# A fused two-model block on one core: the first microseconds and the last block of rows rearranged

## The reference

```python
h = h + 0.5 * swiglu(rms_norm(h, ffn1_norm[li]), ffn1_wi[li], ffn1_wo[li])   # the first FFN, from x
...
x = x + FFN_RESIDUAL_WEIGHT * swiglu_2(rms_norm_2(x, ffn2_norm[l]),          # the last FFN, its result is returned
                                     ffn2_w_gate[l], ffn2_w_up[l], ffn2_w_down[l])
```

## Time and profile before

| what | value |
|---|---|
| median of 3 runs | 1520.33 us |
| profiled execution | 1519.9 us |
| its span, first to last instruction | 1518.1 us |
| mean granted PE clock | 0.993 |
| PE busy | 1486.0 us (98%) |
| DVE busy / ACT busy | 876.0 us (58%) / 710.2 us (47%) |

### The profile page before, as it was taken

One profiled execution on the slowest core, in us unless ns is written; L12 is line 12 of the kernel. 1 busy time (PEld: TensorE's weight loads), 2 busy tenths in 40 slices (PEclk: granted clock), 3 DMA queues, 4 the chain that ended last, 5 costly groups with the idle time before them and its releaser, 6 DMA issues.

```text
span 1518.1 us, 16928 instructions
## 1 busy us (share of the span) xinstructions
PE 1486.0 (98%) x7061; PEld 1234.9 (81%) x7061; DVE 876.0 (58%) x1040; ACT 710.2 (47%) x834; POOL 84.6 (6%) x101
## 2 busy tenths in 40 slices
PE   8999999999999999999799999999999889999999
PEld 6888888888888888888688888888888768888887
DVE  6465456565545655459765554755547786765543
ACT  6444345554434444344554444543436666354432
POOL 0000012000000000006000000000000440000000
PEclk9999999999999999999999999999999999999999
DMA  9555472365555655544455556565556342555552
GB/s 315 177 184 177 133 258 98 130 199 189 194 167 194 194 180 188 173 147 153 138 182 193 173 175 207 181 192 183 180 169 207 124 165 86 194 179 189 187 180 70
DMA packets 143890, 265.66 MB, mean 175 GB/s; under 512 B 7070, under 2 KB 24950, under 8 KB 143558
## 3 DMA queue, kind: packets, MB, share of 16 engines
q1 hardware_dynamic: 141974, 259.11, 52.0%
q0 software_dynamic: 1104, 4.35, 0.9%
q10 hardware_dynamic: 736, 1.12, 0.2%
HBM read 263.52 MB, written 1.05 MB: 174 GB/s over the span
## 4 chain that ended last, share of the span: by engine, by line
PE 89%; DVE 7%; ACT 2%; POOL 1%; issue 1%; POOLq 0%; DVEq 0%; ACTq 0%
PE ps L527 28%; PE ps L529 27%; PE ps L528 27%; PE ps L556 2%; DVE wlo L1468 2%; PE ps L539 1%; PE ps L906 1%; POOL m_qf L2088 0%; ACT whi L1082 0%; PE ps L710 0%; PE ps L1042 0%; PE ps L654 0%; DVE d_i L1796 0%; PE ps L620 0%; DVE d_m L1792 0%
## 5 line engine op out<-in xcount | busy, mean ns | idle before, releaser
L1468 DVE TENSOR_TENSOR wlo<-raw,whi 128x2048 fp32r<-128x2048 f32 (+4 forms) x268 | 568.8, 2127 | 434.5 <-ACT whi L1082 434.4
L1082 ACT CAST whi<-raw 128x2048 fp32r<-128x2048 f32 (+4 forms) x268 | 473.5, 1770 | 449.8 <-PE ps L529 449.1
L527 PE MATMUL ps<-whi,xt_hi 128*128 128x512 f32 (+3 forms) x1376 | 535.1, 389 | 5.2 <-DVE wlo L1468 5.2
L529 PE MATMUL ps<-whi,xt_lo 128*128 128x512 f32 (+3 forms) x1376 | 529.1, 385 | 0.0
L528 PE MATMUL ps<-wlo,xt_hi 128*128 128x512 f32 (+3 forms) x1376 | 528.5, 384 | 0.0
L527 PEld LDWEIGHTS ps<-whi,xt_hi 128*128 128x128 f32 x1376 | 259.0, 188 | 56.8 <-issue 4.0
L529 PEld LDWEIGHTS ps<-whi,xt_lo 128*128 128x128 f32 x1376 | 258.9, 188 | 51.4
L528 PEld LDWEIGHTS ps<-wlo,xt_hi 128*128 128x128 f32 x1376 | 259.0, 188 | 48.9
L527 PE MATMUL ps<-whi,yt_hi 128*128 128x512 f32 (+3 forms) x108 | 43.6, 404 | 8.0 <-DVE wlo L1468 6.8
L1108 ACT ACTIVATE junk<-X 128x512 f32<-128x512 f32 x40 | 25.4, 634 | 44.5 <-DVE X L1523 41.1
L529 PE MATMUL ps<-whi,yt_lo 128*128 128x512 f32 (+3 forms) x108 | 42.0, 389 | 0.0
(11 more groups left out here) (381 smaller groups left out, 1586.2 us busy)
## 6 DMA issues: line engine op xcount, KB each, us to landing
raw<-in_ffn_wi SPq DMA_DIRECT2D x79, 1024.0 KB, 5.2
raw<-in_ffn_wo SPq DMA_DIRECT2D x40, 1024.0 KB, 5.0
raw<-in_ffn_w_gate SPq DMA_DIRECT2D x20, 1024.0 KB, 5.1
raw<-in_ffn_w_up SPq DMA_DIRECT2D x20, 1024.0 KB, 5.1
raw<-in_ffn_w_down SPq DMA_DIRECT2D x20, 1024.0 KB, 5.0
raw<-in_w_in SPq DMA_DIRECT2D x14, 1024.0 KB, 5.4
raw<-in_ffn_wi SPq DMA_DIRECT2D x16, 512.0 KB, 4.8
raw<-in_even_w_in SPq DMA_DIRECT2D x8, 1024.0 KB, 5.8
```

Source lines behind the costliest of these rows:

```text
L527: e.matmul(o, h, hi_w, start=i == 0 and j == 0, stop=False)
L529: t = e.matmul(o, l, hi_w, start=False, stop=end and j == nk - 1)
L1082: e.copy(whi[0:n, v % SPLIT, c], raw[0:n, v % RAW, c]).then_inc(s_hi.mark(*[(v, j) for j in js]), 1)
L1468: e.tensor_tensor(wlo[0:n, v % SPLIT, c], raw[0:n, v % RAW, c], whi[0:n, v % SPLIT, c].bitcast(F32), ALU.subtract).then_inc(s_lo.mark(*[(v ...
```

## The change

Four edits. `WARM` is 2 in place of 4. ScalarE gets one small multiplication into a new buffer `ssum0`, right behind its DMA issues and the wait for the zeroed `junk`; its load of the function table goes with it. The last block's products go through a new function `last_steps`: the second half of the rows is multiplied in two column halves of 256, into the two banks of a pair of their own, beginning from zero there. VectorE's `last_add` first adds what the five blocks before have summed for the second half of the rows, then the first half of the rows, then the two column halves; SP stores the two column halves apart.

```diff
-WARM = 4
+WARM = 2
...
+        ssum0 = sb("ssum0", [128, 1])
...
+            for tt in range(2):
+                q.wait_ge(*s_dve["x", "c2", 0, tt])
+                e.dma_start(out[0, 128 * tt:128 * tt + 128, 0:512], X[:, tt, 0:512]).then_inc(s_out.mark((0, tt)), 16)
+            for tt, c0, n in ((0, 0, 512), (1, 0, 256), (1, 256, 256)):
+                q.wait_ge(*s_dve["x", "c2", 1, tt, c0])
+                c = slice(512 + c0, 512 + c0 + n)
+                e.dma_start(out[0, 128 * tt:128 * tt + 128, c], X[:, tt, c]).then_inc(s_out.mark((1, tt, c0)), 16)
+            q.wait_ge(*s_out[1, 1, 256])
...
                 if v == len(plan) - 1:
-                    order = [(j, tt) for tt in range(2) for j in range(nk)]
+                    return last_steps(job, pair, v, k0, nk)
...
+            def last_steps(job, pair, v, k0, nk):
+
+                wd, own = job.width, take("last")
+                for tt, c0, n in ((0, 0, wd), (1, 0, wd // 2), (1, wd // 2, wd // 2)):
+                    o = own.ap[:, c0 // (wd // 2), 0:n] if tt else pair.ap[:, 0, :]
+                    for j in range(nk):
+                        kt = k0 // 128 + j + job.k_off
+                        q.wait_ge(*s_dve[job.key, kt])
+                        q.wait_ge(*s_lo[v, j])
+                        hi_w, lo_w = (w[:, v % SPLIT, j * wd + c0:j * wd + c0 + n] for w in (whi, wlo))
+                        h, l = (a[:, kt, 128 * tt:128 * tt + 128] for a in (job.act.hi, job.act.lo))
+                        e.matmul(o, h, hi_w, start=tt == 1 and j == 0, stop=False)
+                        e.matmul(o, h, lo_w, start=False, stop=False)
+                        t = e.matmul(o, l, hi_w, start=False, stop=j == nk - 1)
...
-                give(d[1].name, s_dve["x", name, 1, 1])
+                if f is not c2:
+                    give(d[1].name, s_dve["x", name, 1, 1])
...
+            q.wait_ge(*s_dve["warm"])
+            e.mul(ssum0[:, :], junk[:, 0:1], 1.0).then_inc(s_act.mark("table"), 1)
             q.wait_ge(*s_dve["g0"])
...
+            def last_add():
+                pair, own = Pair(c2.d[1].name), Pair("last")
+                q.wait_ge(*s_turn["xt", c2.x, 1])
+                q.wait_ge(*s_act["sq", c2.x, 1, 1])
+                for tt, c0, n, o in ((1, None, 512, pair.ap[:, 1, :]), (0, 0, 512, pair.ap[:, 0, :]),
+                                     (1, 0, 256, own.ap[:, 0, 0:256]), (1, 256, 256, own.ap[:, 1, 0:256])):
+                    if c0 is None:
+                        q.wait_ge(*s_mm[c2.d[1].at[4], 1])
+                    else:
+                        q.wait_ge(*s_mm["last", tt, c0])
+                    after_mine()
+                    xs = X[:, tt, 512 + (c0 or 0):512 + (c0 or 0) + n]
+                    e.scalar_tensor_tensor(xs, o, 0.5, xs, ALU.mult, ALU.add).then_inc(s_dve.mark(("x", "c2", 1, tt, c0)), 1)
```

More of the change, by code:

```diff
@@ L528, in steps @@
                     e.matmul(o, h, lo_w, start=False, stop=False)
-                    t = e.matmul(o, l, hi_w, start=False, stop=end and j == nk - 1)
+                    t = e.matmul(o, l, hi_w, start=False, stop=(end or (v == len(plan) - 2 and tt == 1)) and j == nk - 1)
                     if j == nk - 1:
                         t.then_inc(s_mm.mark((v, tt), *([(job.name, tt)] if end else [])), 1)
+            def last_steps(job, pair, v, k0, nk):
[11 more added lines that the diff above has]
+                        t = e.matmul(o, l, hi_w, start=False, stop=j == nk - 1)
+                    names = [("last", tt, c0)]
+                    if c0 + n == wd:
+                        names += [(v, tt), (job.name, tt)]
+                    t.then_inc(s_mm.mark(*names), 1)
             def turn(name, sources, key, kt0):
@@ L1583, in ffn @@
                     unit()
-                add_to_x(name, 1, d[1], 0.5, f.x, rs)
+                if f is c2:
+                    last_add()
+                else:
+                    add_to_x(name, 1, d[1], 0.5, f.x, rs)
                 if f is not c2 and f is not b2:
                     row_scale(name, RS, ("rs", name))
+            def last_add():
[6 more added lines that the diff above has]
+                        q.wait_ge(*s_mm[c2.d[1].at[4], 1])
+                    else:
+                        q.wait_ge(*s_mm["last", tt, c0])
+                    after_mine()
+                    xs = X[:, tt, 512 + (c0 or 0):512 + (c0 or 0) + n]
+                    e.scalar_tensor_tensor(xs, o, 0.5, xs, ALU.mult, ALU.add).then_inc(s_dve.mark(("x", "c2", 1, tt, c0)), 1)
             def second_scale():
```

## The result

| | before | after |
|---|---|---|
| median | 1520.23 us (1520.10 to 1520.34) | 1527.84 us (1525.57 to 1529.17) |
| profiled execution | 1519.9 us | 1529.17 us |
| its span | 1518.1 us | 1527.4 us |
| PE busy | 1486.0 us | 1496.1 us |

The ratio after to before is 1.0049, with an interval of 1.0031 to 1.0066. The change makes the kernel slower by half a per cent; 1515.5 was forecast, with 1519.1 as the upper end.

The account below looks back on a forecast made before the run. PE, busy 98% of the span, was taken as the bound. Gains of 2.7 + 1.6 + 0.55 = 4.85 from 1519.9 gave 1515.05, plus 0.43 for the median: 1515.5 us, range 1514.2 to 1519.1.

Parts of the forecast that it names:

- The part on the table load: At the start, ScalarE's 1.28 us table load ends near 4.9 behind its DMA issues, hidden before it has other work.
- The low clock later: In later stretches at half clock, a net of one short stretch less, -1.6 us, bounds -3.3 to +1.65.
- The start: Up to block 2's first product: first product at 7.9 to 8.2, block 2 at 20.5 instead of 23.24, 2.7 us gained.
- Rival (2): At the start, the clock rises only some 5 us after 8.2; block 2 gains 0.9, total 1518.9 us; chance 0.13.
- The end: In the last block, a shorter last add and smaller last store gain 0.55 us, bounds 0.1 to 0.6.
- 0.03 on slower: Whole kernel: chance 0.03 of being slower by over 0.2%, through a long low clock or new low stretches.
- a long low clock at the start: At the start, a low clock beyond 14.8 us delays block 2; lasting to 20 it gives 1522.4 us; chance 0.04.
- rival (1): In the later stages, the low-clock stretches change nothing in the sum, leaving 2.7 + 0.55, 1517.1 us; chance 0.27.

Follow-up runs that it names:

- after_al: The whole change against the kernel before, with `ssum0` in the half-empty slot of `ssum` so that no other buffer moves: 1517.43 us, ratio 0.9976.
- best: The whole change against the kernel before, `ssum0` in the slot of `ssum`, and 64 unused bytes ahead of `rows0` moving a1's `ht`: 1515.09 us, ratio 0.9967.
- pad32: The kernel before with only the unused buffer `ssum0` declared, moving all buffers behind it by 32 bytes: 1529.04 us, ratio 1.0053.
- a1_al: The kernel before with 64 unused bytes ahead of `rows0`, moving only a1's `ht` and the early buffers: 1519.45 us, ratio 1.0004.
- warm2_al: The kernel before with only `WARM` at 2 in place of 4: 1519.45 us, ratio 0.9995.
- tail_al: The kernel before with only the new tail for the last block, no buffer moved: 1519.89 us, ratio 0.9997.
- moving32: The kernel before with small buffers declared earlier, so `whi` and `wlo` lie at 160 and `xt`, `yt` at 0 modulo 256: 1557.43 us, ratio 1.0242.
- ht64: The kernel before with `RS`, `RF` and `ssum` in one slot, so all buffers behind lie 64 bytes earlier: 1524.19 us, ratio 1.0028.

## Why the prediction was wrong

**The step that failed: `ssum0` was costed at nothing.** The part on the table load prices the instruction and its place in ScalarE's queue, and passes over the buffer that it writes. None of the rows it used could have shown the price; the diff could have raised the question, since a declaration stands in it and all `ht` are declared behind it. The term that is missing is +9.4 us: the buffer moves all six `ht` by 32 bytes, and 1584 down products get 6 ns slower. With it the sum would have been 1515.5 + 9.4 = 1524.9, 2.9 under the result.

The trace of the kernel before held a sign of it, unread: a1's products with `ht` take 392 ns in the kernel before and those of the other five 391, and a1's down stage takes 61.55 where the others take 60.99. Equal work with unequal times was a thing to ask about, and so were the quarters of the 360-column blocks.

The Trainium skill ("SBUF — State Buffer", Operand start alignment) says that an fp32 operand may start at any multiple of 4 bytes, and that this is about legality and not speed. The runs agree with the first (the products ran at 32 off) and put a number to the second: 2.8% of a product.

**The low clock later, -1.6: wrong in sign.** It was put at a net of one short stretch less. After and after_al have one more short stretch in the gla mixer, and between a1's last and a2's first down product they take 1.32 and 1.33 us longer than before. The mla mixer, between c1's and c2's down products, takes 0.59 and 0.48 longer with the same two long stretches on other work. That is +1.9 and +1.8, just beyond the upper bound of +1.65. In best the same two parts are 0.4 and 0.1 shorter than before. The places do get dealt anew, as the prediction said; with bounds on both sides, zero was the better choice. Kernels whose start is that of the kernel before show it as well: pad32 has three short ones (203.7, 213.9, 244.6), a1_al two, and the times of single executions spread by 5 us. So part of the dealing is not set by the program.

**The start, 2.7.** Its steps held in after_al: table load at 3.67 against 3.63, the first cast at 6.35 as forecast, the first product at 7.98 against 7.9 to 8.2, block 2 at 20.28 against 20.5, held by VectorE's low part of x. The gain was 2.96. In after itself the first product came at 8.38, because the last piece of x was there only at 8.04 and not at 7.6, and then the clock was low for 3.4 us. From its first product to block 2's it took 13.25 us, where the kernel before took 11.90, so 1.35 of the 2.96 went and 1.61 was left.

**Rival (2), no rise before the real products**, foresaw the sign (products 0.43 apart) but not the cause. In after the clock rose sooner than forecast, not later: the dummies end at 4.91 against 5.24 in best, and the transposes behind them are at full speed. It fell again during the waits for x. The prediction asked only whether it would rise; that it could fall again, as it did in after behind a stretch of 3.8 us in which PE was busy for 2.09, was no case of its own. The Trainium skill's rule for that rival ("TensorE: Matmul & The Clock Gate", Part 4 on the PE transpose), that in transpose mode the full clock does not engage, is not borne out. From 1241.4 to the rise at 1252.2 PE of the kernel before ran transposes alone, and the eight of `m_kvf` at 1252.42 then took 1.04 us, where those at 1249.17 had taken 1.91. Best's clock rises behind 1.11 us of transposes, but with 3.78 us of dummies ahead of them, so it says less.

**The end, 0.55.** The last add took 0.42 as forecast. The last product started 0.18 later against the work ahead of it and ended 0.07 later, beside the forecast 0.08, and the time behind its start went from 3.56 to 2.89. That makes 0.49. The extra add lay beside PE's work, as said.

**The sum again**, on spans, each term from the products' starts in both traces:

| part | after | after_al |
|---|---|---|
| up to block 2's first product | -1.61 | -2.96 |
| from there to a1's first down product | +0.02 | +0.12 |
| six down stages | +9.44 | 0.00 |
| gla mixer's stretch, a1 to a2 | +1.32 | +1.33 |
| mla mixer's stretch, c1 to c2 | +0.59 | +0.48 |
| end | -0.49 | -0.50 |

The sums are 9.27 and -1.53; the spans, 1527.4 and 1516.6, differ from the 1518.1 of the kernel before by 9.3 and -1.5.

**The chances.** 0.03 on slower stood on one mechanism, a long low clock at the start. A change that adds a buffer should have had a case in which the buffer's place matters. With the buffer's place kept, the forecast ratio of 0.9968 stands just inside the interval of after_al, 0.9966 to 0.9986; so does that of rival (1), 1517.1 or 0.9979. The ratio does not tell these two apart. The trace does not favour the forecast's way there: after_al's profiled execution lost 1.8 us to the later stretches, where 1.6 was to be gained, so a median that fits it would fit by luck.

## What to carry to other kernels

A new buffer is an edit to every buffer declared behind it, however small it is and whoever uses it. Before and after such a change compare the mean of each group of products with the same shape: in a kernel that is 98% PE, 6 ns on each of 1584 products out of some 5780 is half a per cent. Keep the two operands of the large products at the same place modulo 256 bytes (here it was 128 for both, and no other common place was tried), put small values into slots that are half empty, and take a gain of 0.2% from ten executions and not from three that agree.

## What the runs showed of the hardware

Where stationary and moving operand lie in a partition, against each other or each by itself, sets the pace of fp32r products of 512 columns. They follow each other by 227 ns when both lie at the same place modulo 256 (128 in all these runs), by 232 to 234 (medians) at a distance of 32, and by 231 or 232 at 128 (a1 of ht64). At 64 three products in a row take 687 ns together, but as 232, 226 and 229 in a2 of ht64 and as 229, 231 and 226 in a1 of the kernel before (medians), so no pace belongs to one of the three. Moving the moving operand or the stationary one by 32 does the same. With 360 columns it is 160 ns at the same place and 165 to 167 at 32, 64 and 96.

The granted clock's first change comes at different times in executions of nearly the same start (5.7 us in pad32, 6.4 in the kernel before, 4.45 in after, 6.75 in best), and the stretches at the low level differ in place and length. One fell at the start in after, warm2_al, tail_al and moving32, and not in the others. What deals them was not settled.
